# FFN down projections as pairs of seven products over the inner tiles, with the next group's first up pair ahead of them

## What is computed

```python
def swiglu(x, w_gu, w_down):
    g, u = jnp.split(x @ w_gu, 2, axis=-1)
    return (jax.nn.silu(g) * u) @ w_down

x = x + FFN_RES_WEIGHT * swiglu(rmsnorm(x, norm_ffn1_g[l]), ffn1_w_gu[l], ffn1_w_down[l])
x = x + hybrid_mixer(...)
x = x + FFN_RES_WEIGHT * swiglu(rmsnorm(x, norm_ffn2_g[l]), ffn2_w_gu[l], ffn2_w_down[l])
```

## Time and profile before

| | us |
|---|---|
| median of 3 runs | 1753.06 (1752.43 to 1754.81) |
| the profiled execution, its own time | 1753.69 |
| its span, first to last instruction | 1751.5 |

### The profile page before, as it was taken

How to read it: one execution, slowest core, us unless ns; L and a number is a source line. 1 busy time by engine, 2 the same in 40 slices (tenths; PEclk the granted TensorE clock), 3 DMA queues, 4 the chain that set the end, 5 groups by cost and what they waited for, 6 DMA issues and landing times.

```text
span 1751.5 us, 26596 instructions
## 1 busy us (share of the span) xinstructions
PE 1745.0 (100%) x10407; PEld 1535.1 (88%) x10407; DVE 1180.3 (67%) x1843; ACT 847.4 (48%) x1442; POOL 135.4 (8%) x150
## 2 busy tenths in 40 slices
...
PEclk9999999999999999999999999999999999999999
...
GB/s 184 89 166 176 145 151 151 111 106 85 53 85 107 114 151 177 175 108 98 95 149 140 168 150 150 173 100 131 141 61 61 85 96 138 127 145 141 142 139 72
DMA packets 92618, 220.65 MB, mean 126 GB/s; under 512 B 10800, under 2 KB 12080, under 8 KB 92496
## 3 DMA queue, kind: packets, MB, share of 16 engines
...
...
## 4 chain that ended last, share of the span: by engine, by line
PE 97%; DVE 1%; ACT 0%; issue 0%; DMA 0%; DVEq 0%; ACTq 0%; POOLq 0%
PE ps L2083 19%; PE ps L2085 19%; PE ps L2084 19%; PE ps L2175 10%; PE ps L2177 10%; PE ps L2176 10%; PE ps L2105 2%; PE ps L2107 2%; PE ps L2106 2%; PE ps L2324 0%; PE ps L2454 0%; PE ps L2479 0%; PE ps L2465 0%; PE ps L2327 0%; PE ps L2312 0%
## 5 line engine op out<-in xcount | busy, mean ns | idle before, releaser
L2083 PE MATMUL ps<-Ahi,wh 128*128 128x512 f32 x913 | 357.1, 391 | 0.0
L2084 PE MATMUL ps<-Alo,wh 128*128 128x512 f32 x913 | 355.3, 389 | 0.0
L2085 PE MATMUL ps<-Ahi,wl 128*128 128x512 f32 x913 | 355.3, 389 | 0.0
L2175 PE MATMUL ps<-BThi,wh 128*128 128x256 f32 x1232 | 340.5, 276 | 0.0
L2176 PE MATMUL ps<-BTlo,wh 128*128 128x256 f32 x1232 | 340.4, 276 | 0.0
L2177 PE MATMUL ps<-BThi,wl 128*128 128x256 f32 x1232 | 340.4, 276 | 0.0
L571 ACT ACTIVATE wh<-raw 128x1024 fp32r<-128x1024 f32 (+1 forms) x206 | 213.1, 1036 | 222.3 <-PE ps L2085 187.9
L1189 DVE TENSOR_TENSOR wl<-raw,wh 128x1024 fp32r<-128x1024 f32 (+1 forms) x206 | 250.2, 1215 | 64.7 <-ACT wh L571 62.7
L2176 PEld LDWEIGHTS ps<-BTlo,wh 128*128 128x128 f32 x1232 | 231.6, 188 | 0.0
L2175 PEld LDWEIGHTS ps<-BThi,wh 128*128 128x128 f32 x1232 | 231.3, 188 | 0.0
L2177 PEld LDWEIGHTS ps<-BThi,wl 128*128 128x128 f32 x1232 | 231.3, 188 | 0.0
...
## 6 DMA issues: line engine op xcount, KB each, us to landing
...
```

The lines of the kernel that those rows point to most:

```text
L2083: pe.matmul(ps, wh[:, c], hi[:, k, :], start=(k == 0), stop=False)
L2084: pe.matmul(ps, wh[:, c], lo[:, k, :], start=False, stop=False)
L2085: last = pe.matmul(ps, wl[:, c], hi[:, k, :], start=False, stop=(k == nb - 1))
L2175: pe.matmul(ps, whi[:, w], bhi, start=(new and kp == 0), stop=False, skip_group_check=not new)
```

## The change

The 8 down rows of groups 0 and 1 become 4 pairs each ("down pairs"), 16 in the two FFNs. Their k halves are the even and the odd tiles of a group (the host reorders `w_down` for that), so each two neighbouring tiles 2kp, 2kp+1 give one kp. The two tiles are written in four quarters into DF or BF; DVE makes the four sums from them (`t_sums`, three instructions), ACT copies the seven blocks to DThi (`t_high`, 128x1792), DVE subtracts to DTlo (`t_low`). For these tiles the copy to Ahi and `a_lo` go. DThi and DTlo of kp 0 and 1 lie where Ahi and Alo are, those of kp 2 and 3 where Hhi and Hlo are, all on multiples of 128 bytes. DVE adds the results of a down pair to X (`x_add`, four; `x_kept`, two) and ACT scales the three taps (`x_tap`). The first up pair of the next group (tile 8, tile 16) goes ahead of the down pairs. Group 2 keeps plain down rows. A pair whose turn also builds a kp (after tiles 7, 9, 11, 13, 15; in FFN2 also 5; in FFN1 the first pair has `t_high` and `t_low` for kp 2) is called a building pair below: 12 in all.

```diff
-    def ffn(name, gu, dn, js):
+    def ffn(f, name, gu, dn, js):
         U0[name] = len(plan)
-        for a, b in FG:
+
+        def ups(a, b):
             for j in range(a, b):
+                UP[f, j] = len(plan)
                 add(gu, j, 0, 8, 7, j >= js)
                 add(gu, FT + j, 0, 8, 7)
+
+        def downs(g):
+            DN[f, g] = len(plan)
             for n in range(KT):
-                add(dn, n, a, b, 7)
+                if g < 2 and n % 2 == 0:
+                    DQ[len(plan)] = len(DQ)
+                add(dn, n, FG[g][0], FG[g][1], 7, g < 2 and n % 2 == 0)
+
+        ups(0, 9)
+        downs(0)
+        ups(9, 17)
+        downs(1)
+        ups(17, 22)
+        downs(2)
...
+    DF, _ = sb("DF", [P, NP + 1, 256], off=oAhi + 28 * KB)
+    DThi, DTlo = ([sb(f"DT{part}{kp}", [P, NP, 256], F32R, off=(oAhi, oHhi)[kp // 2] + (14 * (kp % 2) + at_) * KB)[0]
+                   for kp in range(4)] for part, at_ in (("hi", 0), ("lo", 7)))
     SW3, _ = sb("SW3", [P, T], off=M + 56 * KB)
...
+    def act_blocks(g, kp):
+        return BF if (kp == 3 if g == 0 else kp % 2 == 1) else DF
+    def before_act(f, g, kp):
+        if act_blocks(g, kp) is BF and g == 0:
+            return "bl", 8 * f + 4
+        return "tl", 8 * f + 3 * g + kp
...
+    SEQ = [[("up", j, UP[f, j]) for j in range(JS[f], 9)] + [("dn", k, DN[f, 0] + k) for k in range(0, KT, 2)]
+           + [("up", j, UP[f, j]) for j in range(9, 17)] + [("dn", k, DN[f, 1] + k) for k in range(0, KT, 2)]
+           + [("up", j, UP[f, j]) for j in range(17, 22)] for f in (0, 1)]
...
+            def t_high(g, kp):
+                act.wait_ge(s["ts"], 8 * f + 4 * g + kp + 1)
+                if g == 1:
+                    act.wait_ge(s["pe"], PEN[DN[f, 0] + 6][6])
+                elif kp >= 2:
+                    act.wait_ge(s["pe"], PEN[UP[f, JS[f]] - 1])
+                act.activation(DThi[kp][:, :, :], act_blocks(g, kp)[:, 0:NP, :], ACT.Copy).then_inc(s["th"], 1)
+            def x_tap(p, i):
+                q = DQ[p]
+                b, c, dst, scale = ((0, 0, TA[(5, 8)[q % 2]][:, LEFT], 0.5),
+                                    (1, 1, TA[6][:, (LEFT, RIGHT)[q % 2]], -0.5),
+                                    (0, 2, TA[(5, 8)[q % 2]][:, RIGHT], 0.5))[i]
+                if i == 0 and q > 1:
+                    act.wait_ge(s["dk"], 2 * q - 2)
+                act.wait_ge(s["pe"], PEN[p][c])
+                act.activation(dst, BK[BANK[p][b]][:, LEFT], ACT.Copy, scale=scale).then_inc(s["tp"], 1)
...
+            for i, (kind, j, p) in enumerate(SEQ[f]):
...
+                pair_hi(p, 4)
+                if kind == "up" and j > 16:
+                    pair_a(j - 1)
+                t(p, 0)
+                pair_hi(p, 5)
+                pair_hi(p, 6)
+                t(p, 1)
+                pair_next(v, 0)
+                t(p, 2)
+                if i == 0 and f == 0:
+                    t_high(0, 2)
+                elif last[0] == "up" and last[1] < 16 and last[1] % 2 == 1:
+                    t_high(last[1] // 8, last[1] % 8 // 2)
+                pair_next(v, 1)
...
+            def t_sums(g, kp, step):
+                b11, t1, t2, b21, t3, b22, t4, b12 = (act_blocks(g, kp)[:, c, :] for c in range(8))
+                if step == 0:
+                    j = 8 * g + 2 * kp + 1
+                    dve.wait_ge(s["ev"], EVN[UP[f, j] + 1])
+                    b = act_blocks(g, kp)
+                    own.add(dve.tensor_tensor(b[:, 1:5:3, :], b[:, 0:6:5, :],
+                                              b12.unsqueeze(1).broadcast_to([P, 2, 256]), ALU.subtract))
+                elif step == 1:
+                    own.wait()
+                    own.add(dve.scalar_tensor_tensor(out=t2, in0=t1, scalar=-1.0, in1=b22, op0=ALU.mult,
+                                                     op1=ALU.subtract))
+                else:
+                    own.wait()
+                    dve.scalar_tensor_tensor(out=t4, in0=t2, scalar=-1.0, in1=b21, op0=ALU.mult,
+                                             op1=ALU.subtract).then_inc(s["ts"], 1)
+            def t_low(g, kp):
+                dve.wait_ge(s["th"], 8 * f + 4 * g + kp + 1)
+                dve.tensor_tensor(DTlo[kp][:, :, :], act_blocks(g, kp)[:, 0:NP, :], f32(DThi[kp][:, :, :]),
+                                  ALU.subtract).then_inc(s["tl"], 1)
+            def x_add(p, i):
+                k = UNITS[p][1]
+                b, c, dst, scale = ((2, 3, X[:, k, LEFT], 0.5), (0, 4, X[:, k + 1, RIGHT], -0.5),
+                                    (1, 5, X[:, k, RIGHT], 0.5), (0, 6, X[:, k + 1, LEFT], -0.5))[i]
+                dve.wait_ge(s["pe"], PEN[p][c])
+                dve.scalar_tensor_tensor(out=dst, in0=BK[BANK[p][b]][:, LEFT], scalar=scale, in1=dst,
+                                         op0=ALU.mult, op1=ALU.add).then_inc(s["ev"], 1)
+            def x_kept(p):
+                k, q = UNITS[p][1], DQ[p]
+                dve.wait_ge(s["tp"], 3 * PAIR[p] + 3)
+                dve.wait_ge(s["ev"], EV0[p] + 3)
+                dve.tensor_tensor(X[:, k + 1, RIGHT], X[:, k + 1, RIGHT], TA[6][:, (LEFT, RIGHT)[q % 2]],
+                                  ALU.add).then_inc(s["dk"], 1)
+                dve.tensor_tensor(X[:, k, :], X[:, k, :], TA[(5, 8)[q % 2]], ALU.add).then_inc(s["dk"], 1)
...
+                if j in (2, 4):
+                    t_low(0, j // 2 - 1)
...
+                if j % 2 == 1:
+                    for step in range(3):
+                        t_sums(0, j // 2, step)
...
+            for i, (kind, j, p) in enumerate(SEQ[f]):
...
+                if last[0] == "up":
+                    product(last[2], last[1])
+                elif last[0] == "dn":
+                    x_add(last[2], 3)
+                pair_lo(p, 4)
+                if kind == "up" and j > 16:
+                    dve.wait_ge(s["ev"], EV0[UP[f, j - 1]] + 4)
+                    a_lo(22 * f, j - 17, TA[4])
+                if due:
+                    t_sums(*tile, 0)
+                pair_lo(p, 5)
+                if due:
+                    t_sums(*tile, 1)
+                pair_lo(p, 6)
+                if due:
+                    t_sums(*tile, 2)
+                if v in PAIR:
+                    pair_lo(v, 0)
+                    total(v, 0)
+                if kind == "up":
                     merge(p, 0, TA[2][:, LEFT])
+                else:
+                    x_add(p, 0)
+                if v in PAIR:
+                    pair_lo(v, 1)
+                if kind == "up":
                     dve.wait_ge(s["ev"], EV0[p])
                     merge(p, 1, TA[1][:, RIGHT])
+                else:
+                    x_add(p, 1)
+                if i == 0 and f == 0:
+                    t_low(0, 2)
+                elif due:
+                    t_low(*tile)
+                if v in PAIR:
+                    pair_lo(v, 2)
+                else:
+                    lo(v)
+                if kind == "up":
                     merge(p, 2, TA[2][:, RIGHT])
+                else:
+                    x_add(p, 2)
+                if v in PAIR:
+                    pair_lo(v, 3)
+                    total(v, 1)
+                else:
+                    lo(v + 1)
+                if kind == "dn":
+                    x_kept(p)
...
+            if p in DQ:
+                return DThi[kp][:, c, :], DTlo[kp][:, c, :]
...
+                    if p in DQ and c == 0 and UNITS[p][1] == 0:
+                        pe.wait_ge(s["tl"], 4 * (DQ[p] // 4) + kp + 1)
...
+            for kind, j, p in SEQ[f]:
+                pair(p)
...
+        order[a:b] = list(range(a, b, 2)) + list(range(a + 1, b, 2))
+    return np.ascontiguousarray(w[:, :, order, :])
```

More of the change, by code:

```diff
@@ L82 @@
 TZ = {}
+UP = {}
+DN = {}
+DQ = {}
 def _units():
@@ new lines, in pair_a @@
+            def pair_a(j):
+                act.wait_ge(s["ev"], EV0[UP[f, j]] + 4)
+                act.activation(Ahi[:, j - 16, :], TA[4], ACT.Copy).then_inc(s["ah"], 1)
+            def t_high(g, kp):
[5 more added lines that the diff above has]
+                act.activation(DThi[kp][:, :, :], act_blocks(g, kp)[:, 0:NP, :], ACT.Copy).then_inc(s["th"], 1)
@@ new lines, in ffn @@
+            for j in range(JS[f]):
+                u = UP[f, j]
+                kp = j - JS[f] + 5
+                if f == 0 and j == 0:
+                    hi(3)
+                    hi(4)
+                    hi(5)
+                    norm(1)
+                elif j == 0:
+                    hi(u + 2)
+                    act.wait_ge(s["ss"], 21)
+                    sums_hi(SS[:, :], Ahi)
+                    hi(u + 3)
+                    norm(6)
+                silu(u, j)
+                if f == 0 and j < 3:
+                    hi(6 + j)
+                elif j == JS[f] - 1:
+                    pair_hi(u + 2, 2)
+                    pair_hi(u + 2, 3)
+                elif j == JS[f] - 2:
+                    pair_hi(u + 4, 0)
```

(42 more changed lines are left out.)

315 lines of the change are left out of this document (122 added, 193 removed).

## The result

The changed kernel takes 1757.76 us (median of 10 runs, 1754.38 to 1758.63) against 1752.87 (10 runs, 1752.32 to 1754.81): ratio 1.0023, 95% interval 1.0014 to 1.0033. The forecast was 1746.7, and its range ended at 1755. The profiled execution took 1756.08, its span is 1754.3, 2.8 us more than before; the median execution is 1.7 us slower still, and no trace of one is at hand.

The account below looks back on a forecast made before the run. The prediction took PE's matmuls to bound the kernel. Its terms, -13.0 + 1.8 + 1.1 + 3.1 = -7.0 us, took the profiled 1753.69 to 1746.7 us, with a range of 1737 to 1755.

Parts of the forecast that it names:

- Down pairs, -13.0: On PE, sixteen down pairs at 10.08 us replace 32 down rows of 174.3 us in all: 13.0 us saved.
- The choice between 120 and 113.3 ns: Price of a 128x256 matmul in down pairs: 120 ns taken, saving 13.0 us; 113.3 would save 22.0.
- Building pairs, 0.15 each: PE waits 0.15 us on each of the 12 building pairs, 1.8 us in all.
- (b): In building pairs, t_low delays merge 2 and the next pair's first tap, leaving no room at its product 2.
- Plain tiles of FFN1, "DVE has room": Before FFN1's first pair DVE has room for the new work, so no PE wait was counted there.
- (c): In FFN1 pairs 7 and 8 both build; merge 1 comes late in pair 8: 1.1 us of wait, once.
- FFN2's first pair, 3.1: DVE leaves FFN2's plain tiles late, so PE waits 2.1 us, then 1.0 more: 3.1 us, at most 4.4.
- the wait at product 6 (1.0): In FFN2's first pair, merge 1 is done late, holding PE 1.0 us more after its wait at product 2.
- rival 3: Slower: t_high and t_low hold PE in every building pair, 23.5 us lost against 13.0 saved: 1764.2 us; chance 0.12.
- rival 4, "given back": Waits of 0.75 us per building pair, 13.2 us in all, cancel the saving: 1753.9 us; chance 0.12.

Follow-up runs that it names:

- e1: Changed kernel with DF, DThi and DTlo moved by 64 bytes, wh and wl by 128: 1769.65 us, ratio 1.0108 to the kernel before.
- e5: Changed kernel with DF, DThi and DTlo moved by 192 bytes, wh and wl by 256: 1751.24 us, ratio 0.9985 to the kernel before.
- e4: Changed kernel with t_low behind merge 2 (or x_add 2) instead of ahead of it: 1754.21 us, ratio 1.0009 to the kernel before.
- e14: Changed kernel with DT moved except kp 0, tile 17's banks changed, DVE and ACT work reordered, BF and DF swapped in FFN2: 1736.97 us, ratio 0.9905.
- e16: The e14 kernel with DVE's sums_of_blocks ahead of the next row's split in the plain tiles: 1734.99 us, ratio 0.9896 to the kernel before.

## Why the prediction was wrong

Point by point, in the profiled execution (the forecast's term, then what it measured):

- **Down pairs, -13.0: right.** 10.08 us each. The choice between 120 and 113.3 ns was right; e1 and e5 show that the start of the tile decides. The rule of N/2.4 + 2.5 (109.2 ns at N = 256; the Trainium skill, same section as above), which the page gives for an isolated matmul, fits none of the three paces of one width seen here, 113.3, 117.8 and 120.
- **Building pairs, 0.15 each: right.** Tiles 11, 13 and 15 of FFN1, each behind a building pair, take 9.67 to 9.69, by the tap that (b) named; e4 removes it. Few others stand free of larger waits: 0.9 in all instead of 1.8.
- **Plain tiles of FFN1, "DVE has room": the step that failed.** DVE's total ahead of the first pair comes at 86.46, 5.1 us later than the 81.40 of before, of which 1.8 is a later start of the whole. I had reckoned FFN2's ledger and not FFN1's, though the same kind of work lands in both: a_lo gone gives nothing, because low_blocks then waits 1.17 us for BThi. DVE of after (two rows), then of before:

```profile
73.22 2.02 DVE L1310 TENSOR_TENSOR BTlo<-BF,BThi 128x1792 fp32r<-128x1792 f32 x1 [1.17 <-ACT BThi L636]
...
86.46 0.69 DVE L1262 TENSOR_TENSOR SS<-sa,raw 128x512 f32<-128x512 f32 x1
```

```profile
81.40 0.68 DVE L1211 TENSOR_TENSOR SS<-sa,raw 128x512 f32<-128x512 f32 x1
```

  Tile 7 lost 2.5 us where the sum had none, 2.1 in three waits (ahead of products 2, 4 and 6), the rest in the first matmul behind each and at the slow pace. Tile 8 lost 1.6 where the sum had 1.1: its wait ahead of product 6 is the 1.1 of (c), the rest is a small wait and the slow pace.
- **FFN2's first pair, 3.1: the delay right, its price mis-sized, 4.2.** ACT's splits between the total and the tap were left out (0.7), and so was the clock, at 0.50 for a product (1.2); the wait at product 6 (1.0) did not come.
- **Left out: the banks of tile 17**, 0.5 in each FFN. The change itself sets these banks, by the line with `at % 7`, and I had not followed them.
- **Left out: the slow pace**, some 3.0 us net in this execution. It was in the trace of before, in the last two and a half pairs of FFN2's first group; two of them:

```profile
912.27:932.05 19.78, 19.78 (x170) 1.00 0.36 95
```

  I had averaged over stages without it. A change that adds small waits adds chances for it; that the changed kernel's times spread over 4.3 us and those of before over 2.5 fits this, and so would the 1.7 us between the profiled and the median execution, which no run shows.
- **Start.** The first 128x512 matmuls ran at half pace until 9.84 us, 1.8 us more. Two of the experiments' profiles (e14, e16) have this too and the others, with the same start of the program, don't, so it differs between executions and is not the change's. Of after, then of before:

```profile
8.14 1.05 PE L2278 MATMUL ps<-Hlo,wh 128*128 128x512 f32 x2
```

```profile
7.32 0.62 PE L2140 MATMUL ps<-Hlo,wh 128*128 128x512 f32 x2
```

Together -13.0 + 0.9 + 4.1 + 4.2 + 1.0 + 3.0 + 1.8 = +2.0, against 2.8 in the span; the other 0.8 lie behind the last matmul. No single term carries the miss: FFN1's DVE and the slow pace are the largest of the change's own. Of the rivals none was right: rival 3 had the right sign, but its place (all building pairs) was wrong; rival 4, "given back", came nearest in size, without its place. What would have told beforehand: to draw up FFN1's ledger as FFN2's, and to follow each wait to the instruction that ends it, through all that stands ahead of it in its engine's list.
